# A two-layer diffusion backbone on one core: where x stands in the load queue, and where the sums of its squares stand in TensorE's program

## The chip, the cores and the metric

The kernel runs on one core of a Trainium2 chip, as one program. The metric is the device time of one execution in microseconds (us). Lower is better.

## The reference

A latent stream x (256 tokens, 2048 channels) passes through two layers; a context stream ctx (256 tokens) feeds the attention of the first. Cut to what the first stage of the kernel computes:

```python
def rms_norm(x, g):
    y = x * lax.rsqrt(jnp.mean(x * x, axis=-1, keepdims=True) + EPS)
    return y * g

def modulate(x, g, shift, scale):
    return rms_norm(x, g) * (1 + scale) + shift

for l in range(2):
    sh1, sc1, g1, sh2, sc2, g2 = jnp.split(silu(c) @ mod_w[l] + mod_b[l], 6)
    if l == 0:
        csh1, csc1, *_ = jnp.split(silu(c_ctx) @ mod_w[0] + mod_b[0], 6)
        pl = modulate(x, norm_mix_g[0], sh1, sc1) @ ev_w_in
        pc = modulate(ctx, norm_mix_g[0], csh1, csc1) @ ev_w_in[:, KV_LO:KV_HI]
        ...   # attention and short convolution, x = x + g1 * (mix @ ev_w_out)
    else:
        ...   # hyena: long convolution by FFT with filters from a small MLP
    x = x + g2 * ffn(modulate(x, norm_ffn_g[l], sh2, sc2), ffn_w1[l], ffn_w2[l])
return rms_norm(x, final_g)
```

## The kernel before, in words

Each engine has one program, written out in order; semaphores tie them together. Activations lie channel-major: a tile holds 128 channels by 256 tokens, 16 of them for x. After a first stage, 93 units of matrix products follow (512 output columns each, weights in four raw slots `w_raw[:, kg, :]` of 1 MB each). The change touches only the first stage, which ends where TensorE (PE) begins the first of these units, `gemm(U_KV, ...)`.

The first stage has three strands of work.

- **Modulation.** The first 4096 columns of mod_w[0] come as eight units of four 1 MB tiles: `mod_block(u)` issues the loads of unit u on SyncE's queue (SP), `mod_rows(u, kg)` multiplies one tile on PE (four products with 2 output rows), ScalarE (ACT) copies the finished row of a unit out (`row_copy(u)`), `mod_turn(u)` transposes it on PE, and VectorE (DVE) adds the bias (`first_modulation(u)`, semaphore `mc_ready`). A tile's slot is free when `mod_rows` of the unit before has read it, and SP waits for that before it issues the next load.
- **Hyena filters.** For four blocks j: ACT makes the decay windows (`windows(j)`: an Abs, a table load, four Exp), PE multiplies `filters(j, tt)`, DVE applies the window (`windowed(j, tt)`), PE transforms (`spectrum(j, parts)`), ACT copies the four results out and stores them (`spectrum_out(j)`, semaphore `kout_ready`, stores to `k_freq` on ACT's own DMA queue).
- **Norms of x (n = 0) and ctx (n = 1).** ACT squares the 16 tiles into four slots and DVE adds each to `sq_sum` (both called `squares_in(n)`; they pace each other). PE sums over channels (`norm_sums(n, bank, a)`), DVE and ACT form the reciprocal root (`norm` on DVE, `norm_root` on ACT, with a table load for Sqrt), PE spreads it over the partitions (`norm_spread(n, out)`), ACT copies it out.

What fixes the order around the change are the queues. ACT's program, written by hand, is:

```python
squares_in(0); spectrum_out(0); row_copy(1)
norm_root(0); norm_spread(0, rstd, acc[2][:, T:2 * T])
windows(1); squares_in(1); row_copy(2); norm_root(1); ...
```

and DVE's:

```python
squares_in(0); first_modulation(0); norm(0, acc[2][:, 16:18])
dve.wait_ge(bc_full, 1)          # norm_spread(0) on PE is done
squares_in(1); windowed(1, 0); first_modulation(1); windowed(1, 1)
first_gains(0); norm(1, acc[3][:, 16:18]); modulate(0, ctx_items(0), 2)
```

Two waits matter besides: `filters(1, tt)` on PE waits for `kout_ready` 2 (tt = 0) or 4 (tt = 1), that is for the first two or all four copies of `spectrum_out(0)`, and `norm_sums(1)` waits for `mc_ready` 2, which `first_modulation(1)` on DVE gives.

Of the kernel before, what the change touches and what calls it, by code (L numbers as in the profile page):

```python
# [33 lines left out]
T = 256  # L34
# [122 lines left out]
def bass_dit_kernel(nc, x_in, ctx_in, vec_in, tab_in, fwd_in, rope_in, inv_in, small_in, fw3_in, decay_in,  # L157
                    mod_first, mod_rest, ffn_w1, ffn_w2, ev_w_in, ev_w_out, od_w_in, od_w_out, out):
    stack = ExitStack()
    with stack:  # L160
# [3 lines left out]
        def sem(name):  # L164
            return stack.enter_context(nc.semaphore(name))
# [33 lines left out]
        acc, aux = ([four[:, i, :] for i in range(4)] for four in (acc4, aux4))  # L199
# [109 lines left out]
        mc_ready = sem("mc_ready")  # L309
# [62 lines left out]
        def _(sp):  # L372
# [4 lines left out]
            def raw_free(u, kg):  # L377

                if kg == 3:
                    sp.wait_ge(row_full, u)  # L380
                else:
                    sp.wait_ge(raw_used, u * 3 + (kg - 2))
# [43 lines left out]
            def mod_block(u, first=False):  # L426

                for kg in range(4):
                    if not first:
                        raw_free(u, kg)  # L430
                    sp.dma_start(w_raw[:, kg, :].rearrange("p (c n) -> p c n", c=4),
                                 mod_first[kg * 512:kg * 512 + 512, START_COLS[u] * 512:START_COLS[u] * 512 + 512]
                                 .rearrange("(c p) n -> p c n", p=P)).then_inc(landed[kg], 16)
# [2 lines left out]
            sp.dma_start(fw3[0:FHID, :, :], fw3_in).then_inc(w3_landed, 16)  # L436
            sp.dma_start(decay[:, :, :], decay_in).then_inc(decay_landed, 16)
            sp.dma_start(fwd_first, fwd_in).then_inc(fwd_landed, 16)
            sp.dma_start(x[:, :, :], x_in).then_inc(x_landed, 16)
            mod_block(1)  # L440
            sp.dma_start(ctx_raw, ctx_in).then_inc(ctx_landed, 16)
            for i in range(2, START):
                mod_block(i)
# [51 lines left out]
            with sp.Fori(1, 4) as q:  # L495
                u = q * 8 + U_F1
# [12 lines left out]
        def _(pe):  # L509
# [101 lines left out]
            def norm_sums(n, bank, a):  # L611

                pe.wait_ge(sq_steps, NORM_STEPS[n])
                for tt in range(2):
                    mm = pe.matmul(bank[:, a + tt:a + tt + 1], sq_sum[:, tt * P:tt * P + P], ones[:, 0:1],
                                   start=True, stop=True)
                mm.then_inc(ms_full, 1)

            def norm_spread(n, out_):
                pe.wait_ge(diag_ready, n + 1)  # L620
                pe.matmul(out_, ones, sq_sum[:, :], start=True, stop=True).then_inc(bc_full, 1)
# [21 lines left out]
            def filters(j, tt):  # L643

                if j:
                    pe.wait_ge(kout_ready, j * 4 - 2 + 2 * tt)
                for i in range(2):
                    mm = pe.matmul(aux[2 * tt + i][:, :], fh[:, i, tt * P:tt * P + P],
                                   fw3[0:FHID, i, j * 512:j * 512 + 512], start=True, stop=True)
                mm.then_inc(h_full, 1)  # L650

            def spectrum(j, parts):
                pe.wait_ge(filt_made, j * 2 + 2)
                for r in parts:
                    for tt in range(2):
                        mm = pe.matmul(aux[r][:, :], fwd_first[:, tt, r * P:r * P + P],  # L656
                                       (f_sum if r < 2 else f_dif)[:, tt, :], start=(tt == 0), stop=(tt == 1))
                    mm.then_inc(kf_full, 1)

            def mod_rows(u, kg):  # L660

                if kg == 0 and u >= 2:
                    pe.wait_ge(row_copied, u - 1)
                pe.wait_ge(landed[kg], u * 16 + 16)
                for kc in range(4):
                    k = 4 * kg + kc
                    mm = pe.matmul(acc[u % 2][32 * kc:32 * kc + 2, :], silu[:, 0, k:k + 17:16],  # L667
                                   w_raw[:, kg, kc * 512:kc * 512 + 512], start=(kg == 0), stop=(kg == 3))
                mm.then_inc(row_full if kg == 3 else raw_used, 1)

            def mod_turn(u):

                pe.wait_ge(row_copied, u + 1)
                if u >= 2:
                    pe.wait_ge(mc_ready, u - 1)
                    pe.wait_ge(rstd_ready, min(u - 1, 2))
                for ft in range(4):
                    mm = pe.matmul(acc[2 + u % 2][:, 2 * ft:2 * ft + 2], rows[:, u % 2, ft * P:ft * P + P], pick,
                                   start=True, stop=True)
                mm.then_inc(row_turned, 1)  # L680
# [9 lines left out]
            for u in range(1, START):  # L690
                j = u // 2
                mod_rows(u, 0)
                if u % 2 == 0:
                    filters(j, 0)
                    mod_rows(u, 1)
                    mod_turn(u - 1)
                    mod_rows(u, 2)
                    filters(j, 1)
                    mod_rows(u, 3)
                else:  # L700
                    if u == 3:
                        norm_spread(1, acc[3][:, T:2 * T])
                    spectrum(j, (0, 1))
                    mod_rows(u, 1)
                    mod_turn(u - 1)
                    spectrum(j, (2, 3))
                    mod_rows(u, 2)
                    mod_rows(u, 3)
                if u == 1:
                    pe.wait_ge(mc_ready, 1)  # L710
                    norm_sums(0, acc[2], 16)
                    norm_spread(0, acc[2][:, T:2 * T])
                if u == 2:
                    pe.wait_ge(mc_ready, 2)
                    norm_sums(1, acc[3], 16)
# [157 lines left out]
        def _(dve):  # L873
# [154 lines left out]
            def modulate(base, items, n_rstd, between=None):  # L1028

                dve.wait_ge(rstd_ready, n_rstd)  # L1030
                for i in range(len(items) + 2):
                    if i < len(items):
                        src, r, g, _, dst, k = items[i]
                        if i >= 4:
                            dve.wait_ge(normed, base + i - 3)
                        STT(out=center(i % 4), in0=src[:, k, :], scalar=g[:, k:k + 1], in1=r[:, :],
                            op0=ALU.mult, op1=ALU.mult).then_inc(xn_ready, 1)
                    if i >= 2:
                        _, _, _, shift, dst, k = items[i - 2]
                        dve.wait_ge(nrm_hi, base + i - 1)  # L1040
                        STT(out=dst[:, k, T:2 * T], in0=center((i - 2) % 4), scalar=shift(k),
                            in1=dst[:, k, 0:T].bitcast(F32), op0=ALU.add, op1=ALU.subtract).then_inc(normed, 1)
                    if i == 9 and between:
                        between()
# [356 lines left out]
        def _(act):  # L1401
# [71 lines left out]
            def modulate(base, items):  # L1473
                for i, (_, _, _, shift, dst, k) in enumerate(items):
                    act.wait_ge(xn_ready, base + i + 1)
                    f(dst[:, k, 0:T], summed[:, i % 4, 1:T + 1], ACT.Identity, bias=shift(k)).then_inc(nrm_hi, 1)
# [276 lines left out]
```

## Time and profile before

| | |
|---|---|
| median of 3 runs | 2466.35 us (2459.8 to 2468.49) |
| the profiled execution | 2463.4 us, its span 2461.6 us |
| PE matmul busy | 2365.6 us, 96% of the span |
| DVE busy | 1828.8 us, 74% |
| ACT busy | 1021.2 us, 41% |
| DMA | 613.80 MB, mean 249 GB/s |

The span is the time from the first to the last instruction of the profiled execution. Busy shares are averages over the whole span; the change is in the first 6% of it, in which the engines stand quite differently, so the rows below are read by time and by engine. In rows of the timeline the first number is the start in us from the span's start, the second the length of the merged piece, and the bracket at the end tells how long the engine was idle before it and what ended that.

### The profile page before, as it was taken

To read this page: it belongs to the slowest core of one execution; us is meant where nothing else is said; L and a number is where in the kernel's file an instruction comes from. 1 tells how busy PE (TensorE), PEld (TensorE's weight loads), DVE (VectorE), ACT (ScalarE), POOL (GpSimd) and SP (SyncE) were. 2 spreads that over 40 slices of the span, in tenths; PEclk is the share of its full clock that TensorE was granted. 3 is DMA by queue.
4 is the path that set the end of the run, shared out by engine and by line. 5 is a ranking of instruction groups with operands and counts; after the bars stand their busy time and mean duration, and the time that the engine had idled before them with its cause. 6 is when DMAs were issued, how large, how long until landed. Compare 5 with 4: busy or idle time off the path is not lost.

```text
span 2461.6 us, 37194 instructions
## 1 busy us (share of the span) xinstructions
PE 2365.6 (96%) x14336; PEld 2056.3 (84%) x14336; DVE 1828.8 (74%) x2444; ACT 1021.2 (41%) x968; POOL 0.2 (0%) x4
## 2 busy tenths in 40 slices
PE   6899799998999999999989999999999999999997
PEld 2369478887888888888889989999788888888887
DVE  3557769998888888888888777875878655665555
ACT  4432334444444444444443223234444444444444
POOL 0000000000000000000000000000000000000000
PEclk7799899998999999999999999999999999999999
DMA  9897178997888888888875566556677555555552
GB/s 349 283 334 285 47 262 326 344 331 252 307 294 310 325 294 306 298 324 305 299 270 176 205 235 212 206 196 203 228 288 266 182 192 198 188 181 195 190 190 101
DMA packets 266041, 613.80 MB, mean 249 GB/s; under 512 B 12208, under 2 KB 12336, under 8 KB 265456
## 3 DMA queue, kind: packets, MB, share of 16 engines
q1 hardware_dynamic: 260992, 602.08, 68.6%
q10 hardware_dynamic: 4912, 9.77, 1.1%
q8 instruction: 102, 1.67, 0.3%
q14 instruction: 35, 0.29, 0.0%
HBM read 605.51 MB, written 6.29 MB: 249 GB/s over the span
## 4 chain that ended last, share of the span: by engine, by line
PE 86%; DVE 7%; DMA 3%; ACT 2%; issue 1%; SPq 0%; DVEq 0%; ACTq 0%
PE acc L578 22%; PE aux L578 21%; PE acc L604 12%; PE aux L604 11%; PE acc L521 10%; PE aux L521 2%; PE aux L656 1%; DMA w_raw<-mod_first 1%; ACT w_hi L1405 1%; DVE w_lo L885 1%; PE aux L829 1%; PE aux L850 1%; DMA w_raw<-od_w_in 1%; PE aux L518 1%; PE acc L667 1%
## 5 line engine op out<-in xcount | busy, mean ns | idle before, releaser
L885 DVE TENSOR_TENSOR w_lo<-w_raw,w_hi 128x2048 fp32r<-128x2048 f32 x372 | 849.9, 2291 | 243.6 <-ACT w_hi L1405 229.0
L1405 ACT ACTIVATE w_hi<-w_raw 128x2048 fp32r<-128x2048 f32 x372 | 710.2, 1912 | 572.4 <-PE acc L521 191.1
L578 PE MATMUL acc<-act_a,w_hi 128*128 128x512 f32 x1216 | 294.8, 395 | 7.2 <-issue 4.5
L578 PE MATMUL acc<-act_b,w_hi 128*128 128x512 f32 x1216 | 290.1, 391 | 0.0
L578 PE MATMUL aux<-act_a,w_hi 128*128 128x512 f32 x1216 | 290.0, 391 | 0.0
L578 PEld LDWEIGHTS acc<-act_a,w_hi 128*128 128x128 f32 x1216 | 226.5, 191 | 53.6 <-issue 5.5
L521 PE MATMUL acc<-act_a,w_hi 128*128 128x256 f32 x1920 | 261.2, 287 | 5.7 <-DVE summed L925 3.0
L578 PEld LDWEIGHTS acc<-act_b,w_hi 128*128 128x128 f32 x1216 | 223.5, 188 | 43.2
L578 PEld LDWEIGHTS aux<-act_a,w_hi 128*128 128x128 f32 x1216 | 223.5, 188 | 43.2
L521 PEld LDWEIGHTS acc<-act_a,w_hi 128*128 128x128 f32 x1920 | 247.2, 194 | 9.2 <-issue 4.5
L578 PE MATMUL aux<-act_b,w_hi 128*128 128x512 f32 x1024 | 244.3, 391 | 0.0
L893 DVE SCALAR_TENSOR_TENSOR m_raw<-m_raw,wide 128x1024 f32<-128x1024 f32 x180 | 218.0, 1220 | 5.0 <-DMA m_raw<-mod_rest 4.7
L578 PEld LDWEIGHTS aux<-act_b,w_hi 128*128 128x128 f32 x1024 | 188.2, 188 | 36.4
L893 DVE SCALAR_TENSOR_TENSOR scr<-scr,wide 128x1024 f32<-128x1024 f32 x140 | 169.3, 1221 | 0.0
L604 PEld LDWEIGHTS acc<-act_a,w_lo 128*128 128x128 f32 x1216 | 155.9, 191 | 5.9
L604 PEld LDWEIGHTS acc<-act_b,w_lo 128*128 128x128 f32 x1216 | 155.9, 191 | 5.9
L604 PEld LDWEIGHTS aux<-act_a,w_lo 128*128 128x128 f32 x1216 | 155.9, 191 | 5.9
L604 PE MATMUL acc<-act_a,w_lo 128*128 128x256 f32 x1216 | 157.7, 283 | 0.0
L604 PE MATMUL acc<-act_b,w_lo 128*128 128x256 f32 x1216 | 157.7, 283 | 0.0
L604 PE MATMUL aux<-act_a,w_lo 128*128 128x256 f32 x1216 | 157.7, 283 | 0.0
L604 PEld LDWEIGHTS aux<-act_b,w_lo 128*128 128x128 f32 x1024 | 131.3, 191 | 5.0
L604 PE MATMUL aux<-act_b,w_lo 128*128 128x256 f32 x1024 | 132.8, 283 | 0.0
(163 smaller groups left out, 1991.9 us busy)
## 6 DMA issues: line engine op xcount, KB each, us to landing
w_raw<-ffn_w SPq DMA_DIRECT2D x256, 1024.0 KB, 7.1
m_raw<-mod_rest SPq DMA_DIRECT2D x180, 512.0 KB, 6.3
scr<-mod_rest SPq DMA_DIRECT2D x140, 512.0 KB, 6.7
w_raw<-od_w_in SPq DMA_DIRECT2D x48, 1024.0 KB, 8.0
w_raw<-ev_w_in SPq DMA_DIRECT2D x36, 1024.0 KB, 9.0
w_raw<-mod_first SPq DMA_DIRECT2D x32, 1024.0 KB, 9.7
w_raw<-ev_w_out SPq DMA_DIRECT2D x16, 1024.0 KB, 9.6
w_raw<-od_w_out SPq DMA_DIRECT2D x16, 1024.0 KB, 5.2
```

Source lines behind the costliest of these rows:

```text
L518: mm = pe.matmul(aux[ft][:, 0:T], w, act_b[:, k, a:a + T], start=start, stop=stop)
L521: return pe.matmul(banks[ft][:, 0:T], w, rhs[:, k, a:a + T], start=start, stop=stop)
L578: return pe.matmul(banks[:, ft, :], w_hi[:, kg % 2, kc * 512 + ft * P:kc * 512 + ft * P + P], rhs[:, k, :], start=(k == 0), stop=False)
L604: mm = pe.matmul(banks[:, ft, 0:T], w_lo[:, kg % 2, kc * 512 + ft * P:kc * 512 + ft * P + P], rhs[:, k, 0:T], start=False, stop=(k == 15))
L656: mm = pe.matmul(aux[r][:, :], fwd_first[:, tt, r * P:r * P + P], (f_sum if r < 2 else f_dif)[:, tt, :], start=(tt == 0), stop=(tt == 1))
L667: mm = pe.matmul(acc[u % 2][32 * kc:32 * kc + 2, :], silu[:, 0, k:k + 17:16], w_raw[:, kg, kc * 512:kc * 512 + 512], start=(kg == 0), stop ...
L829: mm = pe.matmul(aux[ct // 2][:, ct % 2 * T:ct % 2 * T + T], yf[:, r, ct * P:ct * P + P], inv[:, r, :], start=(r == 0), stop=(r == 3))
L850: mm = pe.matmul(aux[r][:, :], fwd[:, tt, r * P:r * P + P], uT[:, tt, :], start=(tt == 0), stop=(tt == 1))
L885: TT(w_lo[:, kg % 2, :], w_raw[:, kg, :], w_hi[:, kg % 2, :].bitcast(F32), ALU.subtract)\
L893: STT(out=raw, in0=raw, scalar=1.0, in1=wide[:, i % 2 * 1024:i % 2 * 1024 + 1024], op0=ALU.mult, op1=ALU.mult, accum_out=m_part[:, i:i + 1 ...
L1405: return act.activation(out_, in_, func, **kw)
```

## The change

Two things move. On SP's queue the load of x (2 MB) goes from ahead of `mod_block(1)` to behind it. In PE's program `norm_sums(0)` and `norm_spread(0)` leave the end of unit 1's pass and go into unit 2's: the sums behind `mod_rows(2, 1)`, the spread behind `mod_turn(1)`. The programs of DVE and ACT are unchanged.

```diff
@@ -436,8 +436,8 @@
             sp.dma_start(fw3[0:FHID, :, :], fw3_in).then_inc(w3_landed, 16)
             sp.dma_start(decay[:, :, :], decay_in).then_inc(decay_landed, 16)
             sp.dma_start(fwd_first, fwd_in).then_inc(fwd_landed, 16)
+            mod_block(1)
             sp.dma_start(x[:, :, :], x_in).then_inc(x_landed, 16)
-            mod_block(1)
             sp.dma_start(ctx_raw, ctx_in).then_inc(ctx_landed, 16)
             for i in range(2, START):
                 mod_block(i)
@@ -693,7 +693,12 @@
                 if u % 2 == 0:
                     filters(j, 0)
                     mod_rows(u, 1)
+                    if u == 2:
+                        pe.wait_ge(mc_ready, 1)
+                        norm_sums(0, acc[2], 16)
                     mod_turn(u - 1)
+                    if u == 2:
+                        norm_spread(0, acc[2][:, T:2 * T])
                     mod_rows(u, 2)
                     filters(j, 1)
                     mod_rows(u, 3)
@@ -706,10 +711,6 @@
                     spectrum(j, (2, 3))
                     mod_rows(u, 2)
                     mod_rows(u, 3)
-                if u == 1:
-                    pe.wait_ge(mc_ready, 1)
-                    norm_sums(0, acc[2], 16)
-                    norm_spread(0, acc[2][:, T:2 * T])
                 if u == 2:
                     pe.wait_ge(mc_ready, 2)
                     norm_sums(1, acc[3], 16)
```

On SP, at the start of the program (`w_raw` are the modulation tiles, `scr` takes ctx), the difference reads, with - for before and + for changed:

```order
 L437 DMA decay<-decay_in 128x4096
 L438 DMA early_b<-fwd_in 128x1024
-L439 DMA x<-x_in 128x4096
 L431 DMA w_raw<-mod_first 128x4x512 x4
+L440 DMA x<-x_in 128x4096
 L441 DMA scr<-ctx_in 128x4096
```

x now stands behind the four tiles of unit 1, directly ahead of ctx.

On PE, from the second half of `spectrum(0, ...)` on (L667 is `mod_rows`, four products a tile; L615 `norm_sums`, L621 `norm_spread`, L648 `filters`, L678 `mod_turn`):

```order
 L656 MATMUL aux<-scr,early_b 128x512 x4
-L667 MATMUL acc<-w_raw,silu 2x512 x8
-L615 MATMUL acc<-tab,sq_sum 128x1 x2
-L621 MATMUL acc<-sq_sum,tab 128x256
-L667 MATMUL acc<-w_raw,silu 2x512 x4
+L667 MATMUL acc<-w_raw,silu 2x512 x12
 L648 MATMUL aux<-fw,late 128x512 x2
 L667 MATMUL acc<-w_raw,silu 2x512 x4
+L615 MATMUL acc<-tab,sq_sum 128x1 x2
 L678 MATMUL acc<-tab,scr 128x2 x4
+L621 MATMUL acc<-sq_sum,tab 128x256
 L667 MATMUL acc<-w_raw,silu 2x512 x4
```

The three products of the norm now stand behind `mod_rows(2, 0)`, `filters(1, 0)` and `mod_rows(2, 1)`, and the spread also behind the turn of unit 1. No instruction is added or removed.

## Rows read from the trace of the kernel before

**Rows 1.** Busy time by stretch (us, PE, PEld, DVE, ACT, POOL, clock, DMA share, GB/s).

```profile
0.00:150.30 150.30, 115.02 (x464) 42.27 (x464) 65.69 (x168) 67.79 (x121) 0.20 (x4) 0.80 0.93 324
```

**Rows 2.** The chain that ended last, pieces between 14 and 81 us.

```profile
14.14 24.54 DMA w_raw<-mod_first
...
58.27 1.05 ACT decay L1405
...
71.82 1.29 DVE m_raw L1092 x2
...
79.31 1.22 PE acc L621 x2
```

**Rows 3.** Issues on SP's queue, timeline around 35 us.

```profile
31.12 3.94 SPq L431 DMA_DIRECT2D w_raw<-mod_first  x1
35.10 2.49 SPq L441 DMA_DIRECT2D scr<-ctx_in  x1
40.76 0.37 SPq L431 DMA_DIRECT2D w_raw<-mod_first  x1
```

**Rows 4.** DMA issues of 31.1, 40.8 and 47.6 us: KB, us to landing.

```profile
w_raw<-mod_first SPq DMA_DIRECT2D x1, 1024.0 KB, 15.6
...
w_raw<-mod_first SPq DMA_DIRECT2D x1, 1024.0 KB, 16.5
...
k_freq<-m_raw ACTq DMA_DIRECT2D x1, 256.0 KB, 6.7
```

**Rows 5.** Busy time by stretch, columns as in group 1, around the change.

```profile
36.00:46.70 10.70, 7.88 (x24) 2.43 (x24) 8.99 (x20) 6.83 (x17) 0.00 (x0) 0.61 1.06 400
46.70:59.80 13.10, 9.90 (x55) 3.79 (x48) 2.75 (x12) 5.67 (x9) 0.00 (x0) 0.93 1.02 396
66.00:78.00 12.00, 11.16 (x37) 3.31 (x37) 10.39 (x26) 5.43 (x11) 0.00 (x0) 0.50 0.78 243
```

**Rows 6.** PE's timeline from 51.6 us.

```profile
51.62 1.90 PE L667 MATMUL acc<-w_raw,silu 128*2 128x512 f32 x16
53.45 0.61 PE L615 MATMUL acc<-tab,sq_sum 128*128 128x1 f32 x4
57.26 0.70 PE L621 MATMUL acc<-sq_sum,tab 128*128 128x256 f32 x2 [3.20 <-DVE sq_sum L1025]
57.89 1.78 PE L667 MATMUL acc<-w_raw,silu 128*2 128x512 f32 x8
59.59 3.78 PE L648 MATMUL aux<-fw,late 64*128 64x512 f32 x4
63.30 1.89 PE L667 MATMUL acc<-w_raw,silu 128*2 128x512 f32 x8
65.12 1.87 PE L678 MATMUL acc<-tab,scr 128*128 128x2 f32 x8
...
74.55 1.01 PE L615 MATMUL acc<-tab,sq_sum 128*128 128x1 f32 x4 [0.23 <-DVE mc L1074]
```

**Rows 7.** ACT's timeline from 36 us.

```profile
36.00 1.34 ACT L1405 ACTIVATE early_b<-x 128x256 f32<-128x256 f32 x4 [1.24 <-DMA x<-x_in]
...
45.92 0.58 ACT L1405 ACTIVATE m_raw<-aux 128x512 f32<-128x512 f32 x1
...
46.99 0.60 ACT L1405 ACTIVATE m_raw<-aux 128x512 f32<-128x512 f32 x1 [0.49 <-ACT m_raw L1405]
...
54.20 1.28 ACT L1405 ACT_TABLE_LOAD   x1
55.49 0.20 ACT L1405 ACTIVATE stat<-stat 128x2 f32<-128x2 f32 x1
...
63.10 7.13 ACT L1405 ACTIVATE early_b<-scr 128x256 f32<-128x256 f32 x16
```

**Rows 8.** DVE's timeline.

```profile
38.25 0.69 DVE L1096 TENSOR_TENSOR scr<-m_raw 128x512 f32<-128x512 f32 x1
...
77.35 0.16 DVE L1014 TENSOR_SCALAR stat<-acc 128x2 f32<-128x2 f32 x1
```

## The prediction

> **What bounds the kernel now.** I first read the busy time by stretch, to see how much of the span the change can reach. The first stage ends at 150.3 us, and in it PE is busy for 115 us, DVE for 66, ACT for 68, and the DMA engines for 93% of the time [rows 1]. None of the four is clearly the bound; the shares hide that it changes hands. So I read the chain of waits, which says what releases what. Up to 38.7 us it is one DMA, the first tile of unit 1 [rows 2]. From there PE carries it to 53.5 us, and then it goes over to the norm of x and does not come back to PE until 79.31 us: the spread of the norm on PE, ACT's windows from 58.27 us, ACT's and DVE's squares of ctx, DVE's windowing from 71.82 us, the norm of ctx, whose spread is at 79.31 us [rows 2]. In this stretch the pieces lie end to end, with no slack: ACT goes straight from copying out the norm of x into the windows, and DVE, straight behind the last square of ctx, into the windowing. The DMA engines, which moved 400 and 396 GB/s between 36 and 60 us, move only 243 between 66 and 78 us [rows 5], because PE takes the tiles late. So the loads bound the stage up to about 57 us, and from 58 to 80 us it is the ACT and DVE strand that starts with the norm of x.
>
> The question is thus when `windows(1)` on ACT starts, which stands behind `norm_root(0)` and `norm_spread(0)` in ACT's queue. Before, it was 58.27 us [rows 2].
>
> **The change, part by part.**
>
> *The loads.* x is 2 MB, which is 5.2 us at 400 GB/s [rows 5]. The queue behind it was full, so unit 1's tiles come 5.2 us earlier, the first at 38.7 - 5.2 = 33.5 us. x lands when unit 1's last tile landed before, since the same bytes have then been moved: 31.12 + 15.6 = 46.7 us [rows 3, 4], against 36.0 us before [rows 7]. SP still issues it in time: even in the place of ctx, at 35.1 us [rows 3], it would be ahead of its turn at 41.5 us. ctx keeps its place.
>
> *PE up to the end of unit 1.* `mod_rows(1, 0)` ended at about 40.7 us and `spectrum(0)` came behind it. Now the latter waits for DVE's windowing, which ends at 38.25 + 0.69 = 38.9 us [rows 8]. PE is 1.7 us ahead from there, and done with unit 1 at 53.5 - 1.7 = 51.8 us [rows 6].
>
> *ACT.* The squares of x start at 46.7 us instead of 36.0. DVE now waits beside them, as for ctx, where ACT's sixteen squares took 7.13 us [rows 7]: ACT is free at 53.8 us. The second copy of `spectrum_out(0)` ends 46.99 + 0.60 - 45.92 = 1.67 us later [rows 7], at 55.5 us; `filters(1, 0)` waits for it. All four are out, at the same pace, by some 57.6 us, and `row_copy(1)` follows at once.
>
> *The first tile of unit 2.* It landed at 40.76 + 16.5 = 57.3 us [rows 3, 4]. Ahead of it the engines also moved the four stores of `spectrum_out(0)`, 1 MB in all, which are now issued at the earliest at 54.4 us. That is 1 MB less, 2.6 us at 400 GB/s: 54.6 us. (The page DMA: Bandwidth & Descriptors of the Trainium skill, section Queues, rings and completion order, says that an engine takes turns between the queues that have work; by that rule the stores in fact shared with the loads. The trace agrees: a store was down in 6.7 us while a tile issued near it took 12 to 17 [rows 4].)
>
> *PE from there.* With the granted clock at 0.5, as in all of 58 to 78 us before, the steps are those of the rows: from `mod_rows(2, 0)` to `filters(1, 0)` 1.70 us, from there to `mod_rows(2, 1)` 3.71, from there to the end of the row 1.82, `norm_sums` 1.01 [rows 6]. So 54.6, 56.3 (`kout_ready` came at 55.5), 60.0, 61.8, and the sums of x are there at 62.9 us; before it was 53.45 + 0.61 = 54.1 us [rows 6]. The sums come 8.8 us later, and it is mostly PE's queue that makes them late: `mod_rows`, `filters` and `mod_rows` stand ahead of them. DVE has had `sq_sum` since 55.5 us.
>
> *The norm.* Before, 3.2 us passed from the sums to the spread at 57.26 us, with a table load of 1.28 us in it, since ACT had only just finished `row_copy(1)` [rows 6, 7]. Now ACT waits since 58.2 us, so the load is done ahead, as in the norm of ctx, where the same way took 79.31 - 77.35 = 1.96 us [rows 2, 8]. This gives back 1.2 us. (The Trainium skill, page ScalarE: Activation LUTs, section What ACT_TABLE_LOAD costs, has 2.66 us for a switch, the load and a drain behind it; by it 2.7 us would come back and the whole sum be 1.4 us lower. The row decides: the next instruction starts 1.29 us after the load does [rows 7].) The spread starts at 62.9 + 1.96 = 64.9 us, and `mod_turn(1)` in front of it is just done (62.9 + 1.8). At the full clock it took 0.70 us, and ACT was at its windows 1.01 us after its start; at half it takes 1.22 [rows 2, 6], so 1.53 us. `windows(1)` starts at 66.4 us: **66.4 - 58.27 = 8.1 us later**.
>
> *What follows.* The strand from `windows(1)` to the norm of ctx has nothing of PE in it but `filters(1)`, which is done by 71.5 us, and `mod_turn(1)`. It moves by 8.1 us as a whole. PE runs out of work at about 73.5 us, as before, and now stands until 82.6 us, since `norm_sums(1)` waits for DVE (it already did: 0.23 us at 74.55 [rows 6]) and `mod_rows(3, 0)` is queued behind it. SP waits for that in turn, so unit 4's loads come later too: everything from `norm_spread(1)` on is tied to PE's steps and moves by 8.1 us. The gain of the change, a wait of 3.2 us that PE loses at 57.26 us and 3.3 us by which it starts unit 2 earlier, goes into that new wait. After 150.3 us PE is busy for nearly all of the time, and nothing is there to absorb a late start.
>
> Sum: 2463.4 + 8.1 = 2471.5 us for the profiled execution. The runs shown lie at 2459.8, 2466.35 and 2468.49; with the profiled one their middle is about 2465, so I give 2473 us.
>
> **What stays unknown.** PE's clock between 54 and 62 us: half (1.2 GHz) or full (2.4). Before, the mean of 0.93 over 46.7 to 59.8 us [rows 5] puts its fall at about 58 us; PE had run `mod_rows` and the sums to 54.1 us and then stood for 3.2 us [rows 6]. Now PE runs `mod_rows` to 51.8 us and stands until 54.6, so I take half. If it stays full, tiles take 0.95 us and the filters about half of 3.78 (an estimate from the ratio of the `mod_rows` rows): `filters(1, 0)` starts at 55.6, and the second tile, which comes 1 MB and some stores behind the first, at about 58.0 us, is the next wait; the sums are there at 59.5, and the delay is 4.5 us. At the other end the first tile comes no earlier than before, 57.3 us, and the delay is 10.8 us.
>
> **The rivals.**
>
> 1. *The clock stays full* (above): +4.5 us, 2469 us. For it: between 46.7 and 59.8 us it averaged 0.93 [rows 5]. Against it: it was 0.50 from 66 to 78 us with PE 93% busy, so once down it did not rise under these products [rows 5].
> 2. *x itself is late.* The copies of `spectrum_out(0)` are done 8.8 us after x lands, and `filters(1, 0)` can start at 56.3 us; so from a landing of 47.5 us on each us goes into the delay. A landing at 52.7 us, after ctx instead of before it, costs 5.2 us more: 13.3 us, 2478 us. For it: single issues on SP took 3.94 us [rows 3]. Against it: it is issued 6 us ahead of its turn.
> 3. *Faster: the tiles bound the stage, not the norm.* If the strand behind the norm of x had 8 us of slack, unit 2 would start at 54.6 instead of 57.89 us, and the stage would be 3.3 us shorter: 2462 us. For it: PE stands for DMA or the norm ahead of unit 2 and for nothing from there to 74 us [rows 6]. Against it: the chain of waits passes through every piece of that strand and finds no pause in it [rows 2].
>
> **How the numbers follow.** Forecast 0.72 (delay of 6 to 10.8 us), rival 1 0.13, rival 2 0.07, rival 3 or no effect 0.08. 0.3% is 7.4 us, about what a measurement here tells from no change. Of the forecast some two thirds lie above it, as do the cases of rival 2: slower 0.55, same 0.38, faster 0.07. The range, 2464 to 2480, runs from rival 1 less the scatter of the runs shown, to 10.8 us with the same scatter, and leaves out rival 3 and most of rival 2.
>
> **What the profile after would show.** `norm_sums` on x at 62 to 63 us, ACT's Abs (L1405 on `decay`) at 66 instead of 58 us, a wait of PE at 74 to 83 us ended by DVE's `mc`, the ctx spread at 87.4 instead of 79.31, and the first product of `gemm(U_KV)` at 158. The prediction is wrong if the Abs is not over 4 us late, if PE does not wait at 74 us, or if the delay seen at 80 us is gone at 150 us.

## The result

| | median, us | range, runs |
|---|---|---|
| before | 2465.17 | 2459.8 to 2468.98, 12 |
| changed | 2471.56 | 2463.99 to 2475.74, 12 |

The ratio is 1.0021, with a 95% interval of 1.0013 to 1.0029: the change costs 5.2 us (3.2 to 7.1) of 2465. The medians lie 6.4 us apart.

The chain that ended last, in the changed kernel (start, length, what), answers to [rows 2]:

```profile
16.74 13.35 SPq L431
...
32.68 16.53 DMA x<-x_in
...
60.46 0.60 ACT scr L1406
61.07 1.28 ACT L1406
62.37 0.21 ACT stat L1406
...
64.13 1.24 PE acc L621 x2
65.67 1.05 ACT decay L1406
```

The load that carries the chain is no longer unit 1's first tile but x, and from its landing at 49.2 us the chain stays with what ACT's queue paces: the squares (in turn with DVE's additions), four copies, row copy, table load, root. PE appears only for the spread. Its timeline, against [rows 6]:

```profile
56.95 1.04 PE L667 MATMUL acc<-w_raw,silu 128*2 128x512 f32 x8 [2.00 <-DMA w_raw<-mod_first]
58.01 1.98 PE L648 MATMUL aux<-fw,late 64*128 64x512 f32 x4
59.92 1.04 PE L667 MATMUL acc<-w_raw,silu 128*2 128x512 f32 x8
60.89 0.60 PE L615 MATMUL acc<-tab,sq_sum 128*128 128x1 f32 x4
...
64.13 1.22 PE L621 MATMUL acc<-sq_sum,tab 128*128 128x256 f32 x2 [1.74 <-DVE sq_sum L1026]
...
81.94 1.01 PE L615 MATMUL acc<-tab,sq_sum 128*128 128x1 f32 x4 [9.24 <-DVE mc L1075]
...
86.69 1.22 PE L621 MATMUL acc<-sq_sum,tab 128*128 128x256 f32 x2 [1.92 <-DVE sq_sum L1026]
```

Two things are to be seen. The new wait is there, 9.24 us for DVE, behind which `mod_rows(3, 0)` and unit 4's loads are queued. And the products up to 61 us ran at the full clock (1.04 and 1.98 us, not 1.89 and 3.78).

The Abs of the windows is at 65.67 us, 7.4 us after the 58.27 of [rows 2]. Not all of that is the change. The profiled executions differ before they reach anything that was edited:

```profile
32.30 1.06 ACT L1406 ACTIVATE decay<-decay 128x1024 f32<-128x1024 f32 x1 [8.97 <-DMA decay<-decay_in]
```

In the trace of before, this first Abs, which starts when `decay` lands, was at 29.84 us; over the fourteen profiles it lies between 27.8 and 33.3. I call it D and count from it. From D, the windows of block 1 are 4.9 us later (33.37 against 28.43), and the ctx spread too (54.39 against 49.47). D was on average 29.5 us in the five kernels that load x early and 30.9 us in the nine that load it late. So few executions can't tell whether that 1.4 us is chance or part of the change; counting from D hides it if it is. The medians don't settle it: in the last table of the experiments they lie on average 0.1 us above the distance counted from D in the nine, and 0.8 us below it in the four others.

The delay is still there at the end of the stage. The first product of `gemm(U_KV)` is at 158.65 us in the changed kernel and at 150.33 before; from D that is 5.9 us later, in e1 below 3.4.

### The profile page after: what moved, and what is told of

Same layout as the page of the kernel before. It is cut to its first block, busy times and chain, and to the rows that moved or that the text cites. A ratio compares the mean times of both kernels' runs of the same rounds, so it can differ in the third digit from the quotient of the medians.

```text
span 2471.3 us, 37194 instructions
## 1 busy us (share of the span) xinstructions
PE 2365.4 (96%) x14336; PEld 2054.6 (83%) x14336; DVE 1828.1 (74%) x2444; ACT 1020.6 (41%) x968; POOL 0.2 (0%) x4
## 4 chain that ended last, share of the span: by engine, by line
PE 82%; DVE 9%; DMA 3%; ACT 3%; issue 2%; SPq 1%; DVEq 0%; ACTq 0%
PE acc L578 22%; PE aux L578 21%; PE acc L604 11%; PE aux L604 11%; PE acc L521 8%; PE aux L521 2%; DVE w_lo L886 2%; DMA w_raw<-od_w_in 1%; ACT w_hi L1406 1%; PE aux L830 1%; PE aux L656 1%; PE aux L518 1%; DVE summed L1037 1%; PE aux L851 1%; DVE m_raw L894 1%
## 5 line engine op out<-in xcount | busy, mean ns | idle before, releaser
L521 PEld LDWEIGHTS acc<-act_a,w_hi 128*128 128x128 f32 x1920 | 246.6, 194 | 11.5 <-DVE summed L926 4.8
```

What stands on the lines that cost most here:

```text
L521: return pe.matmul(banks[ft][:, 0:T], w, rhs[:, k, a:a + T], start=start, stop=stop)
```

## The experiments

Two theories at first. **A**: ACT's queue behind x sets the start of the windows of block 1, a fixed time after x lands. **B**: PE's queue sets it, because the sums of x stand behind unit 2's products.

Each set of experiments had its own runs of before beside it: 2466.89 us for e1 to e4, 2465.47 for e5 to e8, 2465.01 for e9 to e12. Ratios and differences are to these.

**e1: the changed kernel again.**

> The changed kernel once more, for a second profile beside the first. Theory A (ACT's queue behind x: squares, four copies, a row copy, a table load and the norm must pass before the windows of block 1): the windows' Abs starts 16.4 us after x lands, as in the first profile (49.23 to 65.67 us), and the whole is about 5 us slower than before. Theory B (PE's queue: the sums of x wait behind three groups of unit 2): the Abs follows the sums, whenever x lands; about 62.5 us with the clock full and 66.4 us with it at half. If x lands near 46.7 us here, A gives an Abs at 63.1 us.

2472.11 us, ratio 1.0025 (1.0014 to 1.0037). x landed at 47.34 us and the Abs came at 63.25, 15.9 us later. The table load ended at 60.47 us, just behind the sums (58.99 + 0.61). Here too both strands arrive almost together; this profile doesn't tell A from B.

**e2: only the load moves.**

```diff
-            sp.dma_start(x[:, :, :], x_in).then_inc(x_landed, 16)
             mod_block(1)
+            sp.dma_start(x[:, :, :], x_in).then_inc(x_landed, 16)
```

> Only the load moves; the sums of x stay at the end of unit 1 on PE. A: ACT's queue behind x is as long as in the changed kernel, so the Abs is at x's landing plus 16 us, and the time is +4 to +6 us against before, as with the whole change. B: the sums are no longer behind unit 2's products, they wait for DVE alone (x's landing plus 8.8 us), so the Abs is some 13 us after the landing, near 59.5 us, and the time is +1.5 to +2.5 us.

2471.59 us, 1.0020 (1.0010 to 1.0031): as A said, the same as the whole change. PE had the sums early and then waited for ACT:

```profile
57.80 0.59 PE L615 MATMUL acc<-tab,sq_sum 128*128 128x1 f32 x4 [3.22 <-DVE mc L1074]
63.67 1.22 PE L621 MATMUL acc<-sq_sum,tab 128*128 128x256 f32 x2 [5.29 <-DVE sq_sum L1025]
```

while ACT's queue came only to its root at 61.9 us:

```profile
60.62 1.28 ACT L1405 ACT_TABLE_LOAD   x1
61.91 0.20 ACT L1405 ACTIVATE stat<-stat 128x2 f32<-128x2 f32 x1
```

From landing to Abs: 16.4 us, as in the changed kernel.

**e3: only the sums move.** x is back in its old place.

```diff
-            mod_block(1)
             sp.dma_start(x[:, :, :], x_in).then_inc(x_landed, 16)
+            mod_block(1)
```

> Only the sums move; x is loaded early as before. A: x is not late and ACT's queue is early, so little should be lost: 0 to +2 us. B: the sums stand behind mod_rows(2, 0), filters(1, 0) and mod_rows(2, 1), whose first tile lands at 57.3 us as before (the stores of the spectrum go out early), so the Abs is at 64.8 us (clock full) to 69 us (half): +6.5 to +10.8 us, more than the whole change.

2476.46 us, 1.0050 (1.0032 to 1.0069), over six runs: worse than the whole change, as B said. (By the medians it is +9.6 us, by the ratio about +12; its interval overlaps a little with that of e1, but the profile bears it out: the squares of ctx start 12.1 us later, against 5.5 in e1.) The table load was done at 52.7 us, and the root waited:

```profile
56.50 1.89 PE L667 MATMUL acc<-w_raw,silu 128*2 128x512 f32 x8 [5.78 <-DMA w_raw<-mod_first]
...
65.08 0.20 ACT L1406 ACTIVATE stat<-stat 128x2 f32<-128x2 f32 x1 [12.40 <-DVE stat L1015]
```

So neither theory holds alone. **C**: the windows start at the later of the two strands. Each half of the change lengthens one of them, and their costs (4.7 and 9.6 us) don't add up. The whole even costs less than the sums alone, since the late load also helps PE: unit 2's first tile is 28.7 us after D here and 24.7 and 25.8 us in the two profiles of the changed kernel, and its products ran at half clock here and at the full clock there. That the tile is earlier because the stores of the spectrum are issued later and don't stand ahead of it fits the prediction's sum, but no run tests it; the tile is also issued earlier, 6 us after D instead of 11.

**e4: x behind ctx as well.**

```diff
-            sp.dma_start(x[:, :, :], x_in).then_inc(x_landed, 16)
             sp.dma_start(ctx_raw, ctx_in).then_inc(ctx_landed, 16)
+            sp.dma_start(x[:, :, :], x_in).then_inc(x_landed, 16)
```

> The changed kernel with x behind ctx as well, so that it lands one 2 MB load (5.2 us) later. A: every us of the landing goes into the Abs: +5.2 us against the changed kernel, about +10 us against before. B: the copies of the spectrum hold filters(1, 0) back from x's landing plus 8.8 us = 60.7 us on, so the sums come 4.4 us later than at half clock and nearly as much later at full; against the changed kernel +3 to +5 us. The two are told apart by the profile: A has a fixed 16.4 us from landing to Abs.

2479.11 us, 1.0051 (1.0032 to 1.0069), over six runs: 6 to 7 us above the changed kernel, where A said 5.2 and B 3 to 5. From landing to Abs it was 18.8 us, so A's fixed time failed: PE was the later strand, since `filters(1, 0)` now waited for ACT's copies:

```profile
64.01 3.78 PE L648 MATMUL aux<-fw,late 64*128 64x512 f32 x4 [4.97 <-ACT m_raw L1406]
```

After that wait the filters ran at half clock, which neither theory had in its difference.

**e5: x between the second and the third tile of unit 1**, the rest as changed.

```diff
-            mod_block(1)
+            mod_block(1, kgs=(0, 1))
             sp.dma_start(x[:, :, :], x_in).then_inc(x_landed, 16)
+            mod_block(1, kgs=(2, 3))
```

> The changed kernel with x between the second and the third tile of unit 1, so that it lands 2 MB of tiles (5.2 us) earlier, near 41.5 us. A: the Abs comes 5.2 us earlier, near 58 us, and the time is that of before (within 1 us). B: PE's queue is unchanged, its sums stay behind unit 2's tiles, so nearly the whole loss stays: +4 to +8 us against before.

2476.75 us, 1.0045 (1.0029 to 1.0060), over seven runs: +11.3 us, above the 4 to 8 of B and above the changed kernel. x landed 11.6 us after D instead of 16.9, and nothing came of it; A is refuted here. ACT's table load was over at 55.4 us, and the root waited for DVE until 64.56. PE took the clock's fall:

```profile
55.97 1.89 PE L668 MATMUL acc<-w_raw,silu 128*2 128x512 f32 x8 [2.51 <-DMA w_raw<-mod_first]
57.79 3.78 PE L649 MATMUL aux<-fw,late 64*128 64x512 f32 x4
```

**e6: the changed kernel with ACT's `windows(1)` ahead of `squares_in(0)`**, in its wait for x.

```diff
             windows(0)
+            windows(1)
             squares_in(0)
...
-            windows(1)
```

> The changed kernel with ACT's windows of block 1 ahead of the squares of x, in the 12 us in which ACT waits for x. If the loss goes through the strand norm of x, windows, squares of ctx, norm of ctx, the squares of ctx follow the norm copy at once, 4.8 us earlier (Abs 1.05, table load 1.28, four Exp 2.5): -4 to -5 us against the changed kernel, about the time of before. If the loss is in PE's products or in the loads, the time stays at +5 us.

2467.48 us, 1.0007 (0.9997 to 1.0017): no longer to be told from before, and 2.0 us above it by the medians, where the two sets of the changed kernel had 5.2 and 6.4, and e8, run beside this one, 6.7. The squares of ctx follow the norm at once, with no table load between, so the loss did go through the strand of windows and squares. The gain is 3.2 to 4.4 us, somewhat less than the 4 to 5 expected. In its profile PE's clock fell, and the norm's spread was 34.0 us after D instead of 31.8:

```profile
56.48 3.47 PE L648 MATMUL aux<-fw,late 64*128 64x512 f32 x4
```

**e7: the same move in the kernel before.**

> The kernel before with the same move of the windows. The squares of x then end 1.4 us later on ACT, which nothing waits for until the row copy at 53.6 us. The strand is 4.8 us shorter, but PE's second filters of block 1 are done only at 72.5 us, so DVE's second windowing starts at 72.5 instead of 74.6 us: -2 us against before; -4 if the clock is full at 60 us. If the strand were not the bound: 0.

2460.19 us, 0.9980 (0.9970 to 0.9990): faster than both kernels, and 5.3 us faster than before, where I expected 2. The ctx spread is 47.49 us after D against 49.47, which is the 2 us, and at the end of the stage 0.8 us of it is left; where the rest comes from I can't say from its one profile, an execution of 2464.88 us, the slowest of the twelve.

**e8: eight idle products in PE's new wait.**

```diff
+                    pe.wait_ge(rstd_ready, 1)
+                    for _ in range(8):
+                        pe.matmul(acc[2][:, T:2 * T], ones, tab[:, 0:T], start=True, stop=True)
                     pe.wait_ge(mc_ready, 2)
```

> The changed kernel with eight idle products (128x256, into a bank nobody reads) behind mod_rows(2, 3), in PE's new wait of 9.2 us. They add work and change nothing else. If the wait costs only by its length, the time stays. If it also costs by the clock it leaves, which was at half for the spread and most of the first spectrum behind it (1.22 and 4.94 us against 0.70 and 3.6 at full), the time falls by 1 to 2 us against the changed kernel.

2472.18 us, 1.0029 (1.0018 to 1.0041): nothing gained, where I expected 1 to 2 us. The products ran at the full clock, were over at 73.2 us, and left a wait of 8.2 us; the spread still took 1.22 us and the spectrum 5.27 (5.15 in the same view of the changed kernel). What that clock costs stays open. The run has another use: PE's clock fell in `filters(1, 0)`, and the Abs is 35.2 us after D, 1.8 more than in the profile of the changed kernel.

**e9 to e11: six idle products in the pause ahead of unit 2**, in e5, in the changed kernel, and (in the wait for the norm of x) in the kernel before.

```diff
+                        pe.wait_ge(row_copied, 1)
+                        for _ in range(6):
+                            pe.matmul(acc[0][:, 0:T], ones, tab[:, 0:T], start=True, stop=True)
```

> x between the second and third tile of unit 1, as in e5, and six idle products (128x256, into a bank whose row is already copied) in PE's pause ahead of unit 2. Theory C: the windows start at the later of two strands, x's landing plus 16 us on ACT, and unit 2's products on PE, which are some 4 us shorter at the full clock. Then e5 lost by the half clock, and if the filler keeps it full the Abs comes 3 to 4 us earlier than in e5 (37.5 us after the first Abs on decay there, 33.5 to 34.5 here; 28.4 before), and the time is 3 to 5 us below e5. If the clock is not it, e5's time stays.

> The changed kernel with the same filler. C: ACT's strand of 16 us behind x is the floor, so a full clock on PE brings at most what the runs with a half clock lost: 0 to -2 us against the changed kernel, +4 to +5 us against before. If PE's strand alone decided, the filler would bring nothing where the clock was full anyway (as in two profiles of three) and 4 us where it was not.

> The kernel before with the six idle products in PE's wait for the norm of x (3.2 us at 54.1 us). C: PE's products from 58 to 74 us are not on the strand, so only what stands behind 79 us can gain: the spread and the spectrum at the full clock, up to -2.8 us, if the clock is kept that long; 0 if it is not.

e9: 2471.34 us, 1.0024 (1.0013 to 1.0035). Against its own runs of before it is +6.3 us where e5 is +11.3, but the intervals of the ratios overlap, and the Abs was 36.6 us after D, 0.8 less than in e5 and not 3 to 4: the second tile came late and the clock fell there. C's mechanism is only half shown by it.

```profile
60.34 1.89 PE L668 MATMUL acc<-w_raw,silu 128*2 128x512 f32 x8 [1.74 <-DMA w_raw<-mod_first]
```

e10: 2469.40 us, 1.0015 (1.0006 to 1.0023), +4.4 us, in the range that C gave. PE's products up to the windows ran at the full clock, and the spread still waited 1.53 us for the norm; the Abs came 15.9 us after x landed, which is ACT's strand:

```profile
62.11 0.70 PE L621 MATMUL acc<-sq_sum,tab 128*128 128x256 f32 x2 [1.53 <-DVE sq_sum L1030]
```

e11: 2464.02 us, 0.9995 (0.9986 to 1.0003): no change, as C said. PE's products up to 66 us ran at the full clock, yet PE then only waited longer:

```profile
72.50 1.02 PE L615 MATMUL acc<-tab,sq_sum 128*128 128x1 f32 x4 [6.67 <-DVE mc L1077]
```

**e12: e7 with the filler.**

> The windows of block 1 ahead of the squares of x, in the kernel before, with the filler. In e7 the end of PE's second filters of block 1 had become the next wait: PE had no pause before norm_sums(1). With the full clock at 58 to 72 us these filters end some 5 us earlier, and the rest of the 4.8 us of the strand can come through: -1 to -4 us against e7. If the clock falls all the same: as e7.

2459.75 us, 0.9981 (0.9972 to 0.9990): as fast as e7, so the 1 to 4 us expected did not come, although the clock stayed full and PE's second filters of block 1 were done 7 us earlier from D than in e7. In its profile the stage ends 112.4 us after D, against 120.5 before and 119.7 in e7, but the two medians are 0.4 us apart. The profiled executions of e7 and e12 are themselves 7.1 us apart (2464.88 and 2457.8 us), so these two profiles don't stand for the middle of their runs.

All together, in us from D: x's landing, ACT's first square of ctx (behind the windows, or behind the norm in e6, e7, e12), its distance to before, the same distance at the end of the stage (the first product of `gemm(U_KV)`, 120.5 before), and the difference of the medians.

| kernel | x lands | first square of ctx | to before | end of stage, to before | medians |
|---|---|---|---|---|---|
| before | 6.2 | 33.3 | | | |
| changed | 16.9 | 38.2 | +4.9 | +5.9 | +6.4 |
| e1, again | 18.1 | 38.8 | +5.5 | +3.4 | +5.2 |
| e2, load only | 17.0 | 38.2 | +5.0 | +6.1 | +4.7 |
| e3, sums only | 6.2 | 45.4 | +12.1 | +11.9 | +9.6 |
| e4, behind ctx | 21.9 | 45.6 | +12.3 | +12.7 | +12.2 |
| e5, in the middle | 11.6 | 42.3 | +9.0 | +10.1 | +11.3 |
| e6, windows first | 17.0 | 35.5 | +2.3 | +4.2 | +2.0 |
| e7, before, windows first | | 28.3 | -5.0 | -0.8 | -5.3 |
| e8, filler in new wait | 17.0 | 40.0 | +6.8 | +5.3 | +6.7 |
| e9, e5 and filler | 11.5 | 41.4 | +8.2 | +5.8 | +6.3 |
| e10, changed and filler | 17.0 | 37.7 | +4.4 | +5.2 | +4.4 |
| e11, before and filler | 6.2 | 33.2 | -0.1 | 0.0 | -1.0 |
| e12, e7 and filler | | 27.6 | -5.7 | -8.1 | -5.3 |

The start of ctx's squares in one profile gives the time of the kernel to within 2.6 us in all thirteen, and to within 1 us in nine of them, and in the ten with the windows in their old place the end of the stage keeps that distance to within 2.4 us. That is the strand on which the change works. For e7 and e12 the agreement is not shown by their own traces, which end the stage 0.8 and 8.1 us earlier than before with medians that are both 5.3 us lower.

## Why the prediction was right, and where it was not

- *x lands with unit 1's last tile, unit 2's first tile comes 2.6 us earlier.* Right: forecast 16.9 and 24.8 us after D (46.7 and 54.6 less 29.84), measured 16.9 and 24.7; in e1 18.1 and 25.8. That PE is 1.7 us ahead to the end of unit 1 was only in part so: 1.6 us at the start of the spectrum, 1.0 at the end of the unit. Nothing hung on it, since PE waits there for unit 2's tile.
- *The strand from the norm of x to the norm of ctx has no slack.* Right, and shown both ways: e6 and e7 shorten it and gain, and its delay at the windows, 4.9 us from D, is the same at the ctx spread. It can't be shortened by much alone: in e7 the squares of ctx start 5.0 us earlier and the ctx spread only 2.0, since PE works there without a pause up to the sums of ctx.
- *A new wait of PE for DVE at 74 us.* Right: 9.24 us, from 72.7 us on.
- *The sums come 8.8 us later, and PE's queue makes them late, with PE at half clock.* This is the step that failed in size. From unit 2's first tile to the end of the sums I had 8.3 us (54.6 to 62.9); at the full clock it took 4.5 (56.95 to 61.49), and the sums were there 5.0 us later than before, counted from D. I took half because PE would stand for 2.8 us ahead of the tile. It did stand, for 2.0 to 3.1 us, in the changed kernel's two profiles and in e4, e6 and e8, and the tile still ran at the full clock (1.04 us); in e5, after 2.5 us, it ran at half. In e6 and e8, the same PE program up to there, the clock fell within `filters(1, 0)`. The same PE program meets either clock, and what decides it no run shows. My rival 1 (+4.5 us; its own steps give 4.2 with the spread at the full clock) was nearer to the measured 5.2 than the forecast of 8.1.
- *The table load is done ahead, since ACT waits.* Wrong where the clock is full. The four copies, the row copy and the load end 13.1 us after x lands, and the sums came 0.9 us before that; from the sums to the spread it took 2.6 us and not 1.96. I had ACT's row copy done at 58.2 us, so the load at 59.5; at half clock the sums, at 62.9, are the later. But in rival 1 both fall at 59.5, and I never asked what ACT's strand gives by itself. e2 shows that it costs about 5 us alone. From the rows of before, with four copies of 1.07 us each: 46.7 + 7.1 + 4.3 + 0.6 + 1.3 = 60.0 us for the root, and 2.8 to 3.3 from there to the windows (the spread at full or half clock): +4.5 to +5.0.
- *The delay stays to the end of the stage.* Right in kind: 5.9 and 3.4 us from D in the two profiles. The medians lie 6.4 and 5.2 us above before.
- *The times named for the profile after.* The Abs at 66, the ctx spread at 87.4 and `gemm(U_KV)` at 158 us came within a microsecond (65.67, 86.69, 158.65), and that is luck: `decay` landed 2.46 us later in this execution than in the one before, which made up for most of the 3.2 us by which the delay was forecast too long. In the medians, too: the 6.4 us of this set is the largest measure of the delay (5.2 by the ratio, 5.2 in e1) and brings 2471.56 near to 2473, while 8.1 us lies above the interval of 3.2 to 7.1. I had put the smallest change that can be told at 0.3%; the measured 0.21% is below it, the case "same" to which I gave 0.38, and its interval is still clear of none.
- *Rival 2, x later still.* e4 puts a price on it: +12.2 us, against 13.3 forecast. By my own steps it should have been 12.5: behind ctx x lands at 51.9 us and not at 52.7. The step itself held: `filters(1, 0)` started 8.8 us after x landed.
- *Rival 3, the tiles bound the stage.* Ruled out: PE did start unit 2 earlier, by 3.4 us from D, and the kernel got slower; e7 got faster by shortening the strand alone.

## What to carry to other kernels

Where a value is awaited by several in-order queues, add up each queue to the common point and take the later, and do it for either level of PE's clock: at half clock PE's queue is the later and gave 8 us, at the full clock ACT's is and gives 5. The costs of two edits on parallel strands don't add up (4.7 and 9.6 us apart, 5.2 and 6.4 together), so halves must be measured apart. And an engine that waits for a load is a place for its own later work: the windows moved into ACT's wait were worth 3 to 5 us, with eight table loads in the program instead of ten.

## What was not expected of the hardware

- The start itself varies. The landing of `decay`, issued ahead of every edit, lay between 27.8 and 33.3 us in the fourteen profiles. A difference of single traces of this size must be counted from a common event.
- One issue on SP's queue can last: 13.35 us for a single tile load in the chain above, against 0.38 us for another at 38.36 us. `decay`, issued before it, landed 2.2 us after it ended. What holds such an issue is not shown.
- Idle products kept PE's clock up. Between 50 and 62 us the granted clock (last column but two) was 0.84 in the kernel before and 1.00 in e11, which only adds six products in a pause of 3.2 us:

```profile
50.00:62.00 12.00, 8.80 (x37) 2.80 (x36) 1.73 (x9) 7.26 (x11) 0.00 (x0) 0.84 1.04 388
```

```profile
50.00:62.00 12.00, 10.40 (x66) 5.13 (x62) 2.15 (x10) 8.38 (x15) 0.00 (x0) 1.00 1.05 389
```

  The window lies 2 us later from D in e11, but the same products say it too: unit 2's first tile took 1.04 us in e11 and 1.78 before, 1.04 in e12 and 1.89 in e7, 1.04 in e9 and 1.89 in e5. In e11 it was worth nothing, since PE was not the bound.
